# Two blocks of a transformer in fp32: ring order, the rotation's engine, operands in pairs, and products of a constant tile at layer beginnings

## The reference, cut to what matters

```python
# first block, per layer
h = rms_norm(x, norm_w[layer]);  proj = h @ w_in[layer]          # 5376 columns
q = partial_rope(q, positions);  k = partial_rope(k, positions)   # 16 of 64 dims of 8+2 heads
a = sliding_window_attention(q, k, v, sinks) * silu(z)
o = hgrn2_recurrence(silu(q_h), kin, i_h, logf);  b = rms(o) * w * silu(g_h)
x = x + (sigmoid(gate_attn) * (a @ w_up_attn) + sigmoid(gate_hgrn) * (b @ w_up_hgrn)) @ w_out
# second block, per layer: mod = silu(c) @ ada_w + ada_b
h = x * (1 + sc_t) + sh_t;  y = mixer(h)                          # s0, s2
x = layer_norm(ALPHA * x + (1 + g_t) * y) 
h = x * (1 + sc_c) + sh_c;  y = square(relu(h @ w1)) @ w2         # s1, s3
x = layer_norm(ALPHA * x + (1 + g_c) * y)
```

## Time and profile before

| what | value |
|---|---|
| median of the runs | 1302.39 us |
| profiled execution, its time | 1302.41 us |
| profiled execution, span from first to last instruction | 1300.7 us |
| mean granted TensorE clock | 0.913 |
| TensorE matmuls / VectorE / ScalarE / GpSimd busy | 1109.9 / 490.6 / 547.9 / 746.5 us |
| `wlo` on GpSimd (L810) | 304 times, 727.4 us |
| `whi` on ScalarE (L887) | 304 times, 312.6 us |
| ring loads of ada units | 48 of 1024 KB |

### The profile page before, as it was taken

How to read it: one execution, slowest core, us unless ns; L and a number is a source line. 1 busy time by engine, 2 the same in 40 slices (tenths; PEclk the granted TensorE clock), 3 DMA queues, 4 the chain that set the end, 5 groups by cost and what they waited for, 6 DMA issues and landing times.

```text
span 1300.7 us, 15904 instructions
## 1 busy us (share of the span) xinstructions
PE 1109.9 (85%) x6584; PEld 939.7 (72%) x6584; DVE 490.6 (38%) x689; ACT 547.9 (42%) x748; POOL 746.5 (57%) x341
## 2 busy tenths in 40 slices
PE   4897988877978898699687999999789566999995
PEld 4786867666866676488565988886777455998994
DVE  4557352427572614144646201105300745201014
ACT  3555463335553643244442444443334433444441
POOL 4665554645654555365014788785558015788883
PEclk9898988988988988889798999999799567999997
DMA  5753533465535323863207567676596004565650
GB/s 203 247 182 139 194 114 114 172 217 198 191 128 177 115 97 130 289 214 99 97 13 246 187 235 256 229 244 212 207 337 230 33 0 130 174 198 179 195 163 32
DMA packets 101023, 221.58 MB, mean 170 GB/s; under 512 B 11361, under 2 KB 17879, under 8 KB 94807
## 3 DMA queue, kind: packets, MB, share of 16 engines
q1 hardware_dynamic: 95776, 210.29, 47.1%
q10 hardware_dynamic: 5174, 10.28, 2.2%
HBM read 219.48 MB, written 1.07 MB: 170 GB/s over the span
## 4 chain that ended last, share of the span: by engine, by line
PE 68%; DVE 12%; ACT 7%; DMA 6%; issue 4%; POOL 2%; SPq 0%; ACTq 0%; POOLq 0%; DVEq 0%
PE lin_ps L322 12%; PE lin_ps L323 12%; PE lin_ps L324 12%; PE tmp_ps L329 5%; PE tmp_ps L330 5%; PE tmp_ps L331 5%; PE tmp_ps L420 3%; PE lin_ps L329 2%; PE lin_ps L331 2%; PE lin_ps L330 2%; POOL wlo L810 2%; DMA ring<-in_w_in 2%; DMA ring<-in_b_w_in 2%; PE tmp_ps L517 2%; PE tmp_ps L377 2%
## 5 line engine op out<-in xcount | busy, mean ns | idle before, releaser
L810 POOL TENSOR_TENSOR wlo<-ring,whi 128x1024 fp32r<-128x1024 f32 (+2 forms) x304 | 727.4, 2404 | 439.6 <-ACT whi L887 437.3
L887 ACT CAST whi<-ring 128x1024 fp32r<-128x1024 f32 (+2 forms) x304 | 312.6, 1034 | 551.1 <-PE lin_ps L324 257.2
L322 PE MATMUL lin_ps<-whi,hThi 128*128 128x512 f32 (+2 forms) x528 | 215.0, 407 | 43.4 <-POOL wlo L810 11.5
L323 PE MATMUL lin_ps<-wlo,hThi 128*128 128x512 f32 (+2 forms) x528 | 209.6, 397 | 0.0
L324 PE MATMUL lin_ps<-whi,hTlo 128*128 128x512 f32 (+2 forms) x528 | 209.2, 396 | 0.0
L322 PEld LDWEIGHTS lin_ps<-whi,hThi 128*128 128x128 f32 x528 | 105.9, 201 | 76.3 <-issue 20.0
L329 PE MATMUL tmp_ps<-hThi,whi 128*128 128x256 f32 x520 | 149.9, 288 | 8.5 <-DVE hTlo L1534 8.5
L330 PE MATMUL tmp_ps<-hTlo,whi 128*128 128x256 f32 x520 | 149.1, 287 | 0.0
L331 PE MATMUL tmp_ps<-hThi,wlo 128*128 128x256 f32 x520 | 148.9, 286 | 0.0
L329 PE MATMUL lin_ps<-hThi,whi 128*128 128x256 f32 x352 | 104.2, 296 | 21.0 <-DVE hTlo L1176 9.0
L324 PEld LDWEIGHTS lin_ps<-whi,hTlo 128*128 128x128 f32 x528 | 105.5, 200 | 21.1
(11 more groups left out here) (245 smaller groups left out, 1475.8 us busy)
## 6 DMA issues: line engine op xcount, KB each, us to landing
ring<-in_mlp_w SPq DMA_DIRECT2D x64, 1024.0 KB, 5.3
ring<-in_ada_w SPq DMA_DIRECT2D x48, 1024.0 KB, 5.5
ring<-in_w_in SPq DMA_DIRECT2D x40, 1024.0 KB, 5.9
ring<-in_b_w_in SPq DMA_DIRECT2D x12, 1024.0 KB, 6.7
ring<-in_w_out SPq DMA_DIRECT2D x8, 1024.0 KB, 5.1
ring<-in_a_w_in SPq DMA_DIRECT2D x6, 1024.0 KB, 6.1
ring<-in_w_up_hgrn SPq DMA_DIRECT2D x4, 1024.0 KB, 5.9
ring<-in_w_up_attn SPq DMA_DIRECT2D x4, 1024.0 KB, 5.1
```

Of the source, the lines that this page charges most:

```text
L322: pe.matmul(ps, xh, hi, start=first, stop=False, skip_group_check=True)
L323: pe.matmul(ps, xh, lo, start=False, stop=False, skip_group_check=True)
L810: pool.tensor_tensor(wlo[:, n % PARTS, :, 0:width], ring[:, u % RING, 2 * h:2 * h + 2, 0:width], whi[:, n % PARTS, :, 0:width].bitcast(F32 ...
L887: act.copy(whi[:, n % PARTS, :, 0:width], ring[:, u % RING, 2 * h:2 * h + 2, 0:width]).then_inc(S("high_formed"), 1)
```

## The change

It has four parts. (1) *Ring order.* `reserve` names a layer's first two units before the boundary's `ada`, so they stand ahead of the ada units in the ring; `take_halves` then takes the reserved ones. The boundary's `ada(4)` becomes `ada(2, close=False)`, and the missing ones follow inside s0 (behind its first products and behind s0q0) and s2 (behind every projection, six in all). `ada_close` moves: in the output of an f layer ahead of its last part, and in s0 behind s0q0. (2) *Rotation* goes from VectorE to GpSimd, behind the `wlo` of level 3's first half. (3) *Operands in pairs.* ScalarE and VectorE hand over two k at a time, at every turned operand, and TensorE waits k by k. (4) *Products of a constant tile.* `keep_busy` puts n matmuls of 512 columns ahead of a layer's transposes, ahead of the wait for its input (`BUSY`), and four more behind them at `mixed`. The tile `warm` is a copy that ScalarE makes at the start.

```diff
+BUSY = {"f0": 14, "f1": 16, "s0": 20, "s1": 28, "s2": 28, "s3": 36}
@@ TensorE
+            def reserve(width, *parts):
+                reserved.append(len(halves))
+                unit(parts, width)
             def take_halves(width, *parts):
-                first = len(halves)
-                unit(parts, width)
+                if reserved:
+                    first = reserved.pop(0)
+                else:
+                    first = len(halves)
+                    unit(parts, width)
...
-            def operand_ready(first, second):
-                pe.wait_ge(*first)
-                rest.append(second)
-            def operand(k0):
-                if k0 and rest:
-                    pe.wait_ge(*rest.pop())
+            def operand_ready(*events):
+                rest.extend(events)
+            def operand(kk):
+                while rest and rest[0][0] <= kk:
+                    pe.wait_ge(*rest.pop(0)[1])
+            def turned(name, kk):
+                return (kk, (S("operand_mid"), bump("operand_mid"))), (kk + 2, read_of(name))
...
+            def transposes(name, pieces, ready=None, busy=0):
                 ps = open_tmp(name).rearrange("p a b -> p (a b)")
+                keep_busy(ps[:, 0:HALF], busy)
+                if ready:
+                    pe.wait_ge(*ready)
...
+            def keep_busy(ps, n):
+                for _ in range(n):
+                    pe.matmul(ps, warm[:, 0:P], warm[:], start=True, stop=True)
...
                 if L:
-                    ada(4)
-                pe.wait_ge(S("f_scaled"), L + 1)
-                feature_major(f"f{L}hT", hs)
-                operand_ready(read_of(f"f{L}hT0"), read_of(f"f{L}hT1"))
+                    reserve_feat(w, F0)
+                    ada(2, close=False)
+                if L == 0:
+                    pe.wait_ge(S("warm"), 1)
+                feature_major(f"f{L}hT", hs, ready=(S("f_scaled"), L + 1), busy=BUSY[f"f{L}"])
+                operand_ready(*turned(f"f{L}hT0", 0), *turned(f"f{L}hT1", 4))
...
                     for c in range(2):
+                        if h and c:
+                            ada_close()
                         linear_part(f"f{L}out{c}", w_out, ...)
...
-            def mixed(name):
+            def mixed(name, first):
+                first()
                 if name in ADA_BOUNDARIES:
-                    ada(4)
-                pe.wait_ge(S(f"{name}x"), 1)
-                feature_major(f"{name}hT", x)
-                operand_ready((S("mixed_low"), bump("mixed")), (S("mixed_low"), bump("mixed")))
+                    ada(2, close=False)
+                feature_major(f"{name}hT", x, ready=(S(f"{name}x"), 1), busy=BUSY[name])
+                keep_busy(lin_ps[:, 0, :], 4)
+                operand_ready(*[(2 * j, (S("mixed_low"), bump("mixed"))) for j in range(4)])
...
+            mixed("s0", lambda: [reserve(*latent(k0)) for k0 in (0, 4)])
...
+            ada(2)
             linear_feat("s0iq", w, 1280, hT)
-            ada_close()
             wait_read("s0ik", "s0iq")
...
                 if i == 0:
                     linear_feat("s0q0", w, 0, hT)
+                    ada(2)
+                    ada_close()
...
             for n in range(2):
                 for part in range(2):
-                    if n or part:
-                        ada(2)
                     linear_feat(f"s2{'qk'[part]}{n}", w, part * D + n * HALF, hT)
+                    ada(2)
             for n in range(2):
-                if n == 0:
-                    ada(2)
                 linear_tok(f"s2v{n}", w, 2 * D + n * HALF, HALF, hT)
+                ada(2)
             ada_close()
@@ GpSimd
+            def rotate(L):
+                lows(halves_at[f"f{L}lv3"][0] + 1, halves_at[f"f{L}lv3"][1])
+                pool.wait_ge(*read_of(f"f{L}kv"))
+                pool.wait_ge(*read_of(f"f{L}q"))
+                pool.wait_ge(S("trig"), 1)
+                for i in range(NT):
...
+                    pool.tensor_tensor(ropet[:, 0], x1, cos, ALU.mult)
...
+                    step(pool.tensor_tensor(ropet[:, 3], x1, sin, ALU.mult))
+                    pool.tensor_tensor(x1, ropet[:, 0], ropet[:, 1], ALU.subtract)
+                    step(pool.tensor_tensor(x2, ropet[:, 2], ropet[:, 3], ALU.add))
+                for i in range(NT):
+                    for a in range(2):
+                        ins = pool.tensor_copy(kdup[:, i, :, a, :], qkv[:, i, K0:V0].rearrange("p (g d) -> p g d", g=2))
+                ins.then_inc(S("f_rope"), 1)
...
             pool.wait_ge(S("f_scaled"), 1)
+            rotate(0)
             rstd("f0h", st[:, 1], st[:, 2], "f0ho")
@@ ScalarE
             def high_of(name, k0, cols=None):
                 ps = flat(full_tmp(name))
+                for j in (0, 2):
...
+                        dst, src = flat(hThi[:, k0 + j:k0 + j + 2, :]), ps[:, j * T:(j + 2) * T]
+                        ins = act.copy(dst, src) if cols is None else act.activation(dst, src, ACT.Copy, scale=cols)
+                    ins.then_inc(S("operand_high"), 1)
...
+            act.wait_ge(S("chunkmask"), 1)
+            act.copy(warm[:], chunkmask[:, 0:HALF]).then_inc(S("warm"), 1)
...
+                        if k == 1:
+                            ins.then_inc(S("mixed_mid"), 1)
@@ VectorE
             def low_of(name, k0, cols=None):
                 ps = flat(full_tmp_of(dve, name))
-                dve.wait_ge(S("operand_high"), bump("operand_low"))
+                for j in (0, 2):
+                    dve.wait_ge(S("operand_high"), bump("operand_low"))
...
+                    if j == 0:
+                        ins.then_inc(S("operand_mid"), 1)
                 read(ins, name)
...
             def mixed(name):
+                for k in range(0, KT, 2):
+                    if k % 4:
+                        dve.wait_ge(*read_of(f"{name}hT{k // 4}"))
+                    else:
+                        dve.wait_ge(S("mixed_mid"), bump("mixed_half"))
+                    whole = flat(hs)[:, k * T:(k + 2) * T]
+                    step(dve.tensor_copy(flat(hThi[:, k:k + 2, :]), whole))
+                    dve.tensor_tensor(flat(hTlo[:, k:k + 2, :]), whole, flat(hThi[:, k:k + 2, :].bitcast(F32)),
+                                      ALU.subtract).then_inc(S("mixed_low"), 1)
```

More of the change, by code:

```diff
@@ L126, in build_program @@
         half = sb("half", [P, NT, 8])
+        warm = sb("warm", [P, HALF], F32R)
         csil = sb("csil", [P, KT, ADA_ROWS])
@@ L368, in feat_units, with reserve_feat @@
                         half_used(mm, name)
+            def reserve_feat(w, c0):
+                for k0 in (0, 4):
+                    reserve(HALF, (slice(0, HALF), win(w, c0, HALF, k0)))
             def linear_feat(name, w, c0, src):
                 feat_units(name, open_lin(name), w, c0, src)
-            def transposes(name, pieces):
+            def transposes(name, pieces, ready=None, busy=0):
                 ps = open_tmp(name).rearrange("p a b -> p (a b)")
+                keep_busy(ps[:, 0:HALF], busy)
+                if ready:
+                    pe.wait_ge(*ready)
                 for n, piece in enumerate(pieces):
@@ L435, in scores, with probabilities @@
                     close_tmp(mm, f"{name}s{n}")
-                def turned(n):
+                def probabilities(n):
                     i, g = quads[n]
@@ L472, in attention @@
                     if lag <= n < len(quads) + lag:
-                        turned(n - lag)
+                        probabilities(n - lag)
                     if n > lag:
@@ L553, in _ @@
                           half=turn_lin[f"f{L}ho"][0])
-                wait_read(f"f{L}bT0")
+                operand_ready(*turned(f"f{L}bT0", 0))
                 for c in range(2):
@@ L559, in _ @@
                 feature_major(f"f{L}aT", hs[:, :, 0:HALF], 4)
-                wait_read(f"f{L}aT0")
+                operand_ready(*turned(f"f{L}aT0", 0))
                 def merged(h):
@@ L593, in mlp @@
             def mlp(name, w1, w2, filled):
-                mixed(name)
+                mixed(name, lambda: reserve_feat(w1, 0))
                 groups = 8
@@ L1217, in ada_close, with ada @@
                          f"adaG{n}")
-            def ada():
-                ada_close()
+            def ada(close=True):
+                if close:
+                    ada_close()
                 name, slab = visits[visited[0]]
@@ L1270, in _ @@
                 if L:
-                    ada()
+                    ada(close=False)
                 else:
@@ L1619, in _ @@
             ins.then_inc(S("s0ckvn"), 1)
-            ada_close()
+            ada()
             for i in range(NT):
@@ L1637, in _ @@
                     dve.wait_ge(S("s0idx_used"), n + 1)
+                    if n == 1:
+                        ada()
+                        ada_close()
             ps = flat(full_tmp_of(dve, "s0ckvT"))
@@ L1690, in _ @@
             affine(1, "s2")
-            for _ in range(4):
```

(1 more changed line is left out.)

97 lines of the change are left out of this document (37 added, 60 removed).

## The result

The changed kernel takes 1287.08 us (median of 4 runs, 1281.38 to 1289.1) against 1302.33 in the same session: ratio 0.9864, 95% interval 0.9832 to 0.9895. In a second session it took 1282.78 against 1305.77: 0.9843, 0.979 to 0.9896. Faster, as forecast, but by 15 to 23 us and not by 38. The first median lies outside the range of 1247 to 1283, the second at its upper edge. The profiled execution of the first session took 1289.1 us, span 1287.4.

The account below looks back on a forecast made before the run. TensorE, busy 85% of the span, was taken to bound the kernel by its work, holes and the half clock after them. Stage terms from -16.7 to +3.5 summed to -38.2: 1302.4 to 1264.2 us, range 1247 to 1283.

Parts of the forecast that it names:

- f0 levels: Layer 0's decay levels: hole of 7.0 us before level 6 and 1.7 of half clock go, less 0.7: -8.0 us.
- f1 beginning, to level 0: First product at +8.8 against 13.6, and 2.3 us lost to half clock go: -7.1 us.
- f1 levels: Layer 1's decay levels: the 7.0 us hole, half clock and the ada closing with its wait leave: -16.7 us.
- s0 to q1's end: Beginning -9.4 us, but the ring makes TensorE wait, so first product to s0q1's end grows +12.9: net +3.5.
- s0 attention, projection: Operands handed over in pairs shorten `project` at s0: -1.1 us.
- s1: Beginning of s1: first product at +12.1 against 16.0, and 2.3 us of clock: -6.2 us.
- s3: Beginning of s3: first product at +12.1 against 14.9, and 1.5 us of clock: -4.3 us.
- the rotation on GpSimd: Before level 3's second half: 16 pieces at 0.45 us, 7.2 in all, fit GpSimd's 7.8 us free; no cost taken.
- Rival C: Levels' factors read two SBUF operands while GpSimd is behind; half the levels' gain stays away: +12, 1276 us; chance 0.12.
- Ring order: Next layer's units before ada units shorten beginnings; at s0, q's units issue late, first product S to S+17.
- Pairs and fillers: Layer beginnings: two-k handovers bring first products to +12.1 in s layers; fillers save half clock, 2.3 us at f1.
- Rival B: Fillers don't hold the clock; all five beginnings pay 1.5 to 2.5 us again: +10, 1274 us; chance 0.14.

Follow-up runs that it names:

- second trace: The changed kernel run once more, unaltered, in a second session: 1282.78 us, ratio 0.9843 against the kernel before.
- the late rotation: The changed kernel with GpSimd rotating q and k behind level 7's first-half multiplications instead of level 3's: 1275.46 us, ratio 0.9784 against the kernel before.
- the split one: Changed kernel, places reserved for f1 alone, GpSimd rotating one tile behind level 3, the other behind 5, copies behind 7: 1258.07 us, ratio 0.9631; again 1258.49.
- the order alone: Changed kernel keeping only the ring's order and moved blocks: rotation on VectorE, TensorE waiting for four of eight, no fillers: 1304.51 us, ratio 0.9991.

## Why the prediction was right and wrong

The steps against the first trace (differences of the table's first two columns, up to rounding):

| step | forecast | measured |
|---|---|---|
| start | +0.6 | +0.6 |
| f0 levels | -8.0 | -1.6 |
| f0 rest | -0.9 | +0.5 |
| f1 beginning, to level 0 | -7.1 | -7.5 |
| f1 levels | -16.7 | -8.9 |
| f1 rest | +0.5 | -0.3 |
| s0 to q1's end | +3.5 | +5.0 |
| s0 attention, projection | -1.1 | +5.6 |
| s1 | -6.2 | -4.0 |
| s2 | +1.5 | +1.1 |
| s3 | -4.3 | -3.8 |
| sum | -38.2 | -13.3 |

**The step that failed is the rotation on GpSimd**, priced as "That just fits; I take nothing". Its own price was right, in part by luck: 7.2 us forecast, 7.0 measured (92.56 to 99.6), but as eight products at 0.35 us and four, beside VectorE's operations with two operands in SBUF, at 0.80, where I had taken 0.45 for each. TensorE was not starved. What I left out is what GpSimd does *behind* it. Using up its slack means that the next four `wlo` run back to back, and I already had the row that prices this for VectorE: 0.23 against 2.40. I applied it to the moved pieces ("each by 0.45 us at most") and not to the `wlo` that they push together. 14.2 of the missing 24.9 us are this step. In the second trace it is 14.5 of 14.6, but only because the others, between -3.4 (the start) and +2.6 (s1), cancel. Rival C named it, at 0.12, and sized it at 12. The Trainium skill, SBUF — State Buffer, "Who interferes with whom", has it as an exclusive lock between VectorE's second port and GpSimd; the 2.8 us per operation agree with it, since each lasts about as long as one `wlo` of 2.7 (10.70 for four). Against the kernel before, the late rotation takes 19.0 us off the levels and the split one 20.6, of the forecast 24.7, so the split one gives back 10.1 of the 14.2. Of the rest about 2 us per layer stay ahead of level 6, which I had taken to be ready in time.

**Ring order.** The mechanism and its size were right, iq at 17.9 us against 17. But I took the reserved places as the source of the short beginnings. Mostly they are not: what shortens them is moving the blocks and closings away, the pairs and the fillers. Reserving gave 2.0 at f1 and 2.7 at s0, and cost 9.5 in s0, 6.9 in s2 and 3.4 in s1 with s2's beginning.

**Pairs and fillers.** The sizes at each beginning were about right, with s1 2.2 us short, 1.0 of it because the fillers behind a late block overran x. I priced them as independent. At s3 they are not, since 1.8 us are lost only with neither; for the whole time the runs leave it open. Rival B didn't come true: all beginnings have clock 1.00. Its rule, from the Trainium skill, TensorE: Matmul & The Clock Gate, Part 4, that a transpose doesn't count as busy the way a matmul does, is not borne out by the kernel without fillers. At s1, s2 and s3 nothing but sixteen transposes ran there between 6.88, 7.39 and 8.97 us of idle time and products at full clock.

**s0's attention** was 5.6 us longer, of which the second trace shows nothing. So the first profiled execution was an unlucky one here, and no step of the forecast is to blame.

## What to carry over

Work moved to an engine's free time isn't free when the engine shares something with the one relieved: price the pile-up behind it, and move it in pieces no larger than the slack between two of its regular jobs. A place kept in a strict queue pays only if what it displaces isn't needed at once; try the move and the reservation apart. And two ways of shortening one wait may replace each other, so undo them together as well as singly. Before one pair of stages becomes a rule, look for a stage that contradicts it.

## What the runs showed of the hardware

- A GpSimd product of 128x80 took 0.35 us by itself and 0.80 beside VectorE's operations with two operands in SBUF (four from 92.56), and a `wlo` 2.38 undisturbed, 2.7 beside them. VectorE's operation of 128x512 took 0.68 by itself, 0.84 beside those products and 2.8 to 2.9 beside a `wlo`. Both sides pay.
- After 6.9 to 9.0 us of idle time and sixteen transposes the next products ran at full clock in four beginnings shown here (the kernel without fillers at s1, s2 and s3, the order alone at s2) and at half in two (the order alone at s3; without fillers at s0, after 4.8 us). The wait behind the transposes, 0.68 to 0.88 and 1.75 us in the first four, 1.74 and 0.68 in the other two, doesn't tell them apart.
- The same program ran the attention of s0 once at a granted clock of 0.71 and once at 0.85.
